# A two-layer hybrid decoder trunk on one core: the first weight unit split in halves by VectorE, and the last rows' order

## What is computed

```python
def rms_norm(x, g):
    y = x * rsqrt(mean(x * x, axis=-1, keepdims=True) + 1e-6)
    return y * g

for l in range(2):
    h = h + token_mixer(rms_norm(h, ln1_g[l]), w_in[l], ...)   # z = u @ w_in: 12 small units, then 16 of gates
    h = h + hier_moe(rms_norm(h, ln2_g[l]), ...)               # top-1 group, top-2 of 32 experts
return rms_norm(h, final_g)
```

## Time and profile before

| | |
|---|---|
| median of 3 runs | 1491.13 us (1489.23 to 1492.70) |
| the profiled execution | 1488.76 us |
| its span, first to last instruction | 1487.0 us |
| TensorE busy | 1401.3 us, 94% of the span |
| VectorE, ScalarE, GpSimd busy | 432.0, 474.9, 493.5 us |
| moved from and to memory | 232 GB/s over the span |
| chain that ended last | TensorE 77%, DMA 17%, VectorE 2%, ScalarE 1%, GpSimd 1% |

### The profile page before, as it was taken

One profiled execution on the slowest core, in us unless ns is written; L12 is line 12 of the kernel. 1 busy time (PEld: TensorE's weight loads), 2 busy tenths in 40 slices (PEclk: granted clock), 3 DMA queues, 4 the chain that ended last, 5 costly groups with the idle time before them and its releaser, 6 DMA issues.

```text
span 1487.0 us, 19004 instructions
## 1 busy us (share of the span) xinstructions
PE 1401.3 (94%) x7518; PEld 979.8 (66%) x7518; DVE 432.0 (29%) x1042; ACT 474.9 (32%) x818; POOL 493.5 (33%) x241
## 2 busy tenths in 40 slices
PE   5999999999999898988899999999999999988986
PEld 5888877788888633333388888777888875333333
DVE  3232544411122311111233335443112142121114
ACT  4522466632331111111244325666223311111112
POOL 3634433456660111111154342335566401111101
PEclk9999999999999799999999999999999998999999
DMA  6522222224375899999963223222243669999996
GB/s 239 197 86 70 87 71 72 71 72 162 106 258 206 334 409 420 419 420 416 389 233 109 78 64 101 77 72 71 71 163 129 238 237 410 415 421 419 420 414 260
DMA packets 128978, 331.22 MB, mean 223 GB/s; under 512 B 16469, under 2 KB 90245, under 8 KB 105336
## 3 DMA queue, kind: packets, MB, share of 16 engines
q1 hardware_dynamic: 120248, 314.28, 55.8%
q0 software_dynamic: 8640, 15.69, 2.8%
HBM read 312.16 MB, written 33.55 MB: 232 GB/s over the span
## 4 chain that ended last, share of the span: by engine, by line
PE 77%; DMA 17%; DVE 2%; ACT 1%; SPq 1%; issue 1%; POOL 1%; POOLq 0%; DVEq 0%; ACTq 0%
PE ps L556 18%; PE ps L557 17%; PE ps L558 17%; PE ps L939 13%; DMA w<-in_w 12%; DMA yb<-y_dram 2%; PE ps L753 2%; DMA x_dram<-hs 1%; PE ps L733 1%; PE ps L741 1%; PE ps L931 1%; DMA xg<-x_dram,toks 1%; PE ps L689 1%; SPq L455 1%; PE ps L850 1%
## 5 line engine op out<-in xcount | busy, mean ns | idle before, releaser
L556 PE MATMUL ps<-uH,ringH 128*128 128x512 f32 x720 | 282.0, 392 | 0.0
L557 PE MATMUL ps<-uL,ringH 128*128 128x512 f32 x720 | 280.5, 390 | 0.0
L558 PE MATMUL ps<-uH,ringL 128*128 128x512 f32 x720 | 280.3, 389 | 0.0
L939 PE MATMUL ps<-w,xT 128*64 128x512 f32 x1024 | 228.0, 597 | 16.0 <-DMA w<-in_w 13.5
L939 PEld LDWEIGHTS ps<-w,xT 128*64 128x64 f32 x1024 | 77.7, 138 | 161.4 <-issue 152.0
L1349 POOL TENSOR_TENSOR ringL<-raw,ringH 128x2048 fp32r<-128x2048 f32 (+1 forms) x31 | 137.9, 4458 | 82.9 <-ACT ringH L1079 82.9
L939 PE MATMUL ps<-w,hT 128*64 128x512 f32 x512 | 127.0, 642 | 31.3 <-DMA w<-in_w 19.5
L556 PEld LDWEIGHTS ps<-uH,ringH 128*128 128x128 f32 x720 | 135.2, 188 | 28.9 <-issue 0.7
L558 PEld LDWEIGHTS ps<-uH,ringL 128*128 128x128 f32 x720 | 135.2, 188 | 28.5
L557 PEld LDWEIGHTS ps<-uL,ringH 128*128 128x128 f32 x720 | 135.3, 188 | 27.6
L1395 POOL TENSOR_TENSOR ringL<-raw,ringH 128x2048 fp32r<-128x2048 f32 x32 | 146.9, 4592 | 5.4 <-ACT ringH L1220 5.4
(11 more groups left out here) (260 smaller groups left out, 2074.0 us busy)
## 6 DMA issues: line engine op xcount, KB each, us to landing
w<-in_w SPq DMA_DIRECT2D x176, 1024.0 KB, 17.9
raw<-in_w_in SPq DMA_DIRECT2D x54, 1024.0 KB, 5.2
w<-in_w SPq DMA_DIRECT2D x32, 512.0 KB, 17.9
braw<-in_w_branch SPq DMA_DIRECT2D x32, 256.0 KB, 4.4
raw<-in_w_out SPq DMA_DIRECT2D x8, 1024.0 KB, 5.2
yb<-y_dram SPq DMA_DIRECT2D x8, 1024.0 KB, 16.0
h_dram<-hs SPq DMA_DIRECT2D x2, 2048.0 KB, 11.3
y_dram<-attT SPq DMA_DIRECT2D x8, 512.0 KB, 8.5
```

The source lines that it names most:

```text
L556: mm(o, h, rh, start=first, stop=False)
L557: mm(o, h, rl_, start=False, stop=False)
L558: return mm(o, l, rh, start=False, stop=last)
L939: ins = mm(o[r], lhs[:, r], rhs[x], start=first, stop=last, skip_group_check=True)
```

## The change

Front: SyncE loads `g1` ahead of weight unit 0. TensorE issues six identity products (`keep_warm(6, 5)`) once `cst` is there, transposes tile 0, issues five more, and starts tile 0's product; the transposes of tiles 1, 2, 3 move to the middle (k = 4) of the products of tiles 0, 1, 2. For unit 0, TensorE waits for the first half of the low part before the product and for the second half only at k = 4. ScalarE makes the high part of unit 0 in two halves of 1024 columns, with `norm_h(0)` and squares 1 between them, and `split_h(2)` comes ahead of `norm_h(3)`. VectorE makes the low part of unit 0 in two halves (`unit_low_half`), GpSimd no longer does. End: the mean of tile 0 is made ahead of tile 1's additions, tile 3's scaling and store are cut in two halves of 512 columns, and TensorE issues four products of banks 2 and 3 ahead of bank 1's wait. Layer 1's front is unchanged.

```diff
--- before.py
+++ after.py
@@ -268,7 +268,7 @@
     bank_filled = signal("bank_filled", NH + 40)
     NB0, NB1 = (NH + 1) // 2, NH // 2
     bank_freed = [signal("bank_freed0", NB0 + 20), signal("bank_freed1", NB1 + 20)]
-    front_high = signal("front_high", 1); front_low = signal("front_low", 1)
+    front_high = signal("front_high", 1, 1); front_low = signal("front_low", 1, 1)
     side_turned = signal("side_turned", 2); side_copied = signal("side_copied", 2)
     lowrank_ready = signal("lowrank_ready", 1)
     decay_arg = signal("decay_arg", 1)
@@ -359,8 +359,8 @@
     def _(sp):
         sp.dma_start(hs[:, 0, :], a["x"][0, 0:P, :]).then_inc(x_in[0].h, 16)
         sp.dma_start(cst[:], a["c_small"]).then_inc(cst_in.h, 16)
+        sp.dma_start(g1[:], a["ln1_g"][0:1, :].partition_broadcast(P)).then_inc(g1_in.h, 16)
         sp.dma_start(raw[:, 0, :].rearrange("p (k n) -> p k n", k=KD), w_in_cols(0, COL["gv"], 256)).then_inc(w_in_slot[0].h, 16)
-        sp.dma_start(g1[:], a["ln1_g"][0:1, :].partition_broadcast(P)).then_inc(g1_in.h, 16)
         for t in range(1, NT):
             sp.dma_start(hs[:, t, :], a["x"][0, t * P:(t + 1) * P, :]).then_inc(x_in[t].h, 16)
 
@@ -542,8 +542,13 @@
         hold(sp, h_out.h, 16 * L)
         for t in range(NT):
             hold(sp, rows_normed.h, rows_normed.at(L, t + 1))
-            sp.dma_start(out[0, t * P:(t + 1) * P, :], ut[:, t, :]).then_inc(s_out.h, 16)
-        hold(sp, s_out.h, 16 * NT)
+            if t < NT - 1:
+                sp.dma_start(out[0, t * P:(t + 1) * P, :], ut[:, t, :]).then_inc(s_out.h, 16)
+        for c in range(2):
+            cc = slice(c * 512, (c + 1) * 512)
+            hold(sp, rows_normed.h, rows_normed.at(L, NT + c))
+            sp.dma_start(out[0, (NT - 1) * P:S, cc], ut[:, NT - 1, cc]).then_inc(s_out.h, 16)
+        hold(sp, s_out.h, 16 * (NT + 1))
 
 
 
@@ -567,7 +572,13 @@
             pe.wait_ge(y_back[t].h, y_back[t].at(lay, 16))
             mm(bank(SUM_BANKS[x]), ident, yb[t][:, 1, cc], start=False, stop=True, skip_group_check=True).then_inc(sum_filled.h, 1)
 
+        def keep_warm(n, b):
+
+            for _ in range(n):
+                mm(bank(b, 256), ident, cst[:, 0:256], start=True, stop=True)
+
         pe.wait_ge(cst_in.h, 16)
+        keep_warm(6, 5)
         for lay in range(L):
 
             def norm_transposes(n, dst_free):
@@ -584,7 +595,7 @@
 
             norm_transposes(0, rows_low)
             if lay == 0:
-                norm_transposes(1, rows_low)
+                keep_warm(5, 5)
             else:
                 token_rows(5, 0, True, False)
                 token_rows(5, 1, False, False)
@@ -592,12 +603,11 @@
                 other_rows(lay - 1, 5)
 
             def second_tile():
-                if lay:
-                    norm_transposes(1, rows_low)
-                    for x in (6, 7):
-                        token_rows(x, 0, True, False)
-                        token_rows(x, 1, False, False)
-                        other_rows(lay - 1, x)
+                norm_transposes(1, rows_low)
+                for x in (6, 7):
+                    token_rows(x, 0, True, False)
+                    token_rows(x, 1, False, False)
+                    other_rows(lay - 1, x)
                 norm_transposes(2, rows_low)
 
             def half(q):
@@ -606,8 +616,9 @@
                 n = UNITS[u][1]
                 wH = ringH[:, s, 0:KD * n].rearrange("p (k n) -> p k n", k=KD)
                 wL = ringL[:, s, 0:KD * n].rearrange("p (k n) -> p k n", k=KD)
-                pe.wait_ge(unit_low.h, unit_low.at(lay, u + 1))
-                if u == 0 and lay:
+                if u or lay:
+                    pe.wait_ge(unit_low.h, unit_low.at(lay, u + 1))
+                if u == 0:
                     pe.wait_ge(front_low.h, front_low.at(lay - 1, 1))
                 if q >= 2:
                     pe.wait_ge(bank_freed[b].h, bank_freed[b].at(lay, q // 2))
@@ -618,14 +629,16 @@
                 else:
                     for i in range(2):
                         if q < 2:
-                            if q == 0 and i == 1:
+                            if q == 0 and i == 1 and lay:
                                 second_tile()
-                            if q == 1 and i == 0 and lay == 0:
-                                norm_transposes(3, rows_low)
                             hold(pe, rows_low.h, rows_low.at(lay, 2 * q + i + 1))
                         for k in range(KD):
                             if q == 1 and i == 0 and k == 4 and lay:
                                 norm_transposes(3, rows_low)
+                            if q < 2 and 2 * q + i < 3 and k == 4 and lay == 0:
+                                norm_transposes(2 * q + i + 1, rows_low)
+                                if q == i == 0:
+                                    pe.wait_ge(unit_low.h, unit_low.at(0, 1))
                             last = mm3(ps[:, b * 512 + i * n:b * 512 + (i + 1) * n], uH[:, k, tmc(2 * off + i)],
                                        uL[:, k, tmc(2 * off + i)], wH[:, k, :], wL[:, k, :], k == 0, k == KD - 1)
                 last.then_inc(bank_filled.h, 1)
@@ -914,15 +927,10 @@
             def list_weights(rhs):
                 return list_product(lambda x: rhs[:, x].rearrange("p a e -> p (a e)"), 384, 2 * NP)
 
-            def keep_warm(n):
-
-                for _ in range(n):
-                    mm(bank(A[0], 256), ident, cst[:, 0:256], start=True, stop=True)
-
-            keep_warm(2)
+            keep_warm(2, A[0])
             pe.wait_ge(list_weights_ready.h, list_weights_ready.at(lay, 1))
             list_weights(w_rhs).then_inc(list_weights_filled.h, 1)
-            keep_warm(6)
+            keep_warm(6, A[0])
 
 
             def transpose_rows(src):
@@ -977,8 +985,11 @@
                 hold(pe, tokens_ready.h, tokens_ready.at(lay, 2))
                 for x in range(2 * NT if lay + 1 == L else 5):
                     if x < 2:
+                        if x and lay + 1 == L:
+                            token_rows(2, 0, True, False)
+                            token_rows(3, 0, True, False)
                         hold(pe, last_low.h, last_low.at(lay, x + 2))
-                    else:
+                    elif lay + 1 < L or x > 3:
                         token_rows(x, 0, True, False)
                     if lay + 1 == L and x < 4:
                         token_rows(x, 1, False, True).then_inc(sum_filled.h, 1)
@@ -1101,11 +1112,13 @@
 
             row_squares(0)
             if lay == 0:
+                act.wait_ge(w_in_slot[0].h, w_in_slot[0].at(0, 16))
+                fn(ringH[:, 0, 0:1024], raw[:, 0, 0:1024], ACT.Copy).then_inc(front_high.h, 1)
+                norm_h(0)
                 row_squares(1)
-                split_h(0)
+                fn(ringH[:, 0, 1024:2048], raw[:, 0, 1024:2048], ACT.Copy).then_inc(unit_high.h, 1)
                 row_squares(2)
                 row_squares(3)
-                norm_h(0)
                 norm_h(1)
             else:
                 norm_h(0)
@@ -1119,6 +1132,7 @@
             split_h(1)
             if lay == 0:
                 norm_h(2)
+                split_h(2)
                 norm_h(3)
 
             def k2_rows(br):
@@ -1158,7 +1172,7 @@
 
             for q in range(NH):
                 kind, u, off, name = HALVES[q]
-                if q == 0 or HALVES[q - 1][1] != u:
+                if (q == 0 and lay) or (q and HALVES[q - 1][1] != u):
                     split_h(u + 2)
                 if name == "ga":
                     act.wait_ge(s_cst.h, 16 * N_CST)
@@ -1354,8 +1368,6 @@
 
             for t in range(NT):
                 norm_scale(t)
-                if lay == 0 and t == 1:
-                    split_l(0)
             split_l(1)
             if lay == 0:
                 hold(pool, s_cst.h, 16 * N_CST)
@@ -1491,10 +1503,27 @@
             v.tensor_tensor(uL[:, :, tmc(t)], ps[:, b * 512:b * 512 + 1024].rearrange("p (k n) -> p k n", k=KD),
                             uH[:, :, tmc(t)].bitcast(f32), ALU.subtract).then_inc(rows_low.h, 1)
 
+        def unit_low_half(c):
+
+            cc = slice(c * 1024, (c + 1) * 1024)
+            if c == 0:
+                dve.wait_ge(front_high.h, front_high.at(-1, 1))
+            else:
+                dve.wait_ge(unit_high.h, unit_high.at(0, 1))
+            v.tensor_tensor(ringL[:, 0, cc], raw[:, 0, cc], ringH[:, 0, cc].bitcast(f32), ALU.subtract).then_inc((front_low, unit_low)[c].h, 1)
+
         mean_square(0, 0)
         first_rows(0, 0)
+        unit_low_half(0)
+        norm_low(0, 0)
         mean_square(0, 1)
         first_rows(0, 1)
+        mean_square(0, 2)
+        unit_low_half(1)
+        first_rows(0, 2)
+        norm_low(0, 1)
+        mean_square(0, 3)
+        first_rows(0, 3)
 
         for lay in range(L):
             links = [0]
@@ -1507,12 +1536,6 @@
 
 
             if lay == 0:
-                norm_low(0, 0)
-                mean_square(0, 2)
```

(13 more changed lines are left out.)

## The result

The changed kernel took 1495.76 us, the median of 11 runs (1492.76 to 1498.80), beside 1490.40 us for the kernel before in 11 runs (1488.26 to 1494.33): a ratio of 1.0036, 95% interval 1.0026 to 1.0046. It is **5.4 us slower**, where 2.9 us faster was forecast; the range ended at 1490.4. The profiled execution took 1494.09 us with a span of 1492.3, against 1488.76 and 1487.0.

A forecast was written before the change was run, and what follows sets the result against it. TensorE, busy without a gap from 36 to 311 us, was taken as the bound, its beginning held by scaled rows and weights. Front 2.1 plus end 0.75 made 2.9 us: 1488.2 against the 1491.13 median, range 1486.2 to 1490.4.

The forecast's parts named there:

- The extra cold identity products: Front: TensorE's identity products ahead of tile 0's product, claimed to cost nothing if they end before 14.8 us.
- they are worth nothing: End: TensorE's four reordered products fill a wait of their own; the banks are full before VectorE asks, so no gain.
- rival 5: Front: TensorE, with waits between tiles, stays at the low clock until tile 3; +6.9 - 0.75, 1497.3 us; chance 0.04.
- Front, 2.1 us: Kernel start: product begins at 14.8 instead of 20.3 us, waits between tiles eat the rest; -2.1 us (-1.6 to -2.6).
- rival 1: Front: GpSimd's factor 2 delays VectorE's second low half by 0.55 us; gain 2.35, 1488.8 us; chance 0.12.
- Rival 3: Front: scaling 3 avoids GpSimd's collision at 1.28 us, tile 2 starts 0.65 earlier; gain 3.55, 1487.6 us; chance 0.10.
- Rival 4: Front: weights or unit 2 land late, each 1 us costing 1 us; at 1.5, 1489.7 us; chance 0.08.
- should arrive at 311 us unchanged: From 36 to 311 us TensorE is busy without a gap, so an earlier beginning should carry through whole.
- End, 0.75 us: Last rows: earlier mean plus halved last scaling and store, -0.75 us together (-0.15 to -0.8).
- The order: End: tile 0's mean ahead of tile 1's additions starts scaling 0 0.2 us earlier, kept to the end.
- The halved store: End: half of the 2.6 us landing is transfer, so halving saves up to 0.65; 0.6 taken, bounds 0 and 0.65.
- rival 2: Front: transposes don't raise the clock, so the product starts 1.9 us late; gain 1.9, 1489.3 us; chance 0.16.

The follow-up runs named there:

- experiment 3: The kernel before with only the front's edits, identity products included, the end as before: 1494.53 us, ratio 1.0024.
- experiment 2: The kernel before with only the edits of the last rows (mean's order, four early products, halved scaling and store), TensorE's code unmoved: 1490.63 us, ratio 0.9998.
- experiment 6: The changed kernel with 64 satisfied waits in layer 0 where TensorE waits for weights, later code moved 106 in all: 1489.87 us, ratio 0.9984.
- experiment 12: The changed kernel with 32 satisfied waits in layer 0 where TensorE waits for weights, later code moved 74 in all: 1493.97 us, ratio 1.0008.
- experiment 7: The changed kernel with six wider identity products instead of eleven, so later code moves by 23 instructions: 1496.32 us, ratio 1.0034.
- experiment 8: Experiment 6 with GpSimd's low half of unit 1 in layer 0 held back until VectorE has scaled tile 3: 1491.77 us, ratio 0.9998.

## Why the prediction was wrong

**The step that failed** is two sentences: "The extra cold identity products cost nothing as long as they end before 14.8", and of the tail, "they are worth nothing". Each was weighed by TensorE's time where the products stand. Neither sum asks what else their instructions change. The first set moves TensorE's code by 43 instructions and brings a jump of about 4 us instead of 0.4 at each of two places, 2.0 us lost in layer 0 and 0.9 in layer 1 (experiment 3; 2.4 in layer 0 of the changed kernel). The second costs nothing in experiment 2, where they fill a wait of 0.76 us for `yL`, and about 2 more in layer 1 once TensorE is late and its clock low. None of the five rivals had this; rival 5, the only one on the slow side, had its reason in the front's clock, which was at the upper level.

The sum from the profiles: front -1.2, tail -0.25, jump of layer 0 +2.4, end of layer 1 +2.8 gives +3.8 against a span that is 5.3 longer. Of the other 1.5, 1.1 lie at the identity products ahead of the experts, which run at the lower level (5.47 us instead of 4.10); that was seen, not tried, and the rest was not traced.

**Front, 2.1 us.** Right in mechanism, and some 0.6 too high: 1.17 in the two profiles compared, 1.5 between the averages. From ScalarE's first instruction on unit 0 to the second bank's copy it is 23.28 us in four profiles, those of the changed kernel and of experiments 3, 6 and 12 (11.84 to 35.12, 11.09 to 34.37, 10.70 to 33.98, 11.71 to 34.99). The forecast has 22.8 (11.2 to the bank's end at 33.8, and 0.2 for the copy); 0.44 of the 0.5 more is VectorE's wait for the factor, which takes 1.36 us instead of 0.55 beside the low half, rival 1's effect. The weights' landing, taken as 11.2, was between 10.6 and 11.8: that is the spread of 0.6 up and down, from 1.2 to 2.3 us of gain, against the one profile of the kernel before, in the profiles with identity products. Rival 3 was mispriced: with the collision missed 0.34 comes back, not 0.65, since `norm_low(2)` then waits for TensorE's transposes. Rival 4's cause (weights late) was in the profiled run with 0.6 of its 1.5 us. The prediction also says that whatever the front gains "should arrive at 311 us unchanged". In the changed kernel it did (1.17 to 498 us); in the profiles of experiments 3, 6 and 7 it did not, about 3 us were lost at 147 to 157 us (last section).

**End, 0.75 us.** 0.25 in its place. The order gave 0.25 as forecast (0.2). The halved store, put at 0.6 by half of a landing of 2.6 us, gave nothing; the low bound of 0 was right. No row showed that half of the landing is transfer. The landing did get 0.5 us shorter with half of the bytes (2.1 us); the later issue and the longer way from landing to end took it back.

**The whole, without the moved code**, is what experiment 6 measures: 0.9984 (0.9972 to 0.9996), 2.4 us by the ratio (0.6 to 4.2; 1.7 by the medians), beside the 2.9 forecast. It is the only kernel that shows a gain: experiment 8, with its code in the same place, has 0.9998 (0.9986 to 1.0010), and in the profile of experiment 6 the front's 2.3 us are gone by 157 us. So a net gain of the change is likely small and not shown beyond doubt; what is shown is that without the stops the change is not slower. The result was wrong by 8 us. The range, built from the bounds of named steps, had no place for a cost that belongs to none. (Added up again, the bounds give 1487.7 to 1489.4 us, not 1487.5 to 1489.3, and rival 2's gain of 1.9 gives 1489.2; neither matters here.) A chance of 0.04 for slower was far too small for a change that puts some forty instructions ahead of 15,000.

## What to carry to other kernels

Count the instructions that a change adds or takes away on each engine, and look for the jumps behind them: a change can pay for itself where it stands and lose more at a jump 700 us later. The sign is an "issue" wait right behind a jump that the kernel before does not have; the proof is the kernel before with satisfied waits in place of the change, put where the engine waits anyway. Try a few shifts before a change is given up: here 0, 9 and 106 did not delay the next squares, and 23 to 74 delayed them by 2.0 to 5.7 us in layer 0 and by 0 to 2.8 in layer 1.

## What the hardware showed besides

- The jump over the empty loop costs 0.4 us with its target's block there and 3 to 5.9 us without; 0 to 4.6 us of that are seen as idle TensorE.
- A wait on a semaphore that has long been reached costs TensorE about 0.16 us (64 of them 10.2 us in experiment 6; each also raised a semaphore).
- Behind a stretch of 2.4 us of idle the granted clock read 0.50, the level of 1.2 GHz, and each product of 512 columns took 0.43 us instead of 0.23 (layer 1 of the changed kernel). In experiments 3, 6 and 7 it also reads 0.51 to 0.53 from 147 to 153.8 us, where TensorE was busy without a gap; the row of experiment 6, with 32 matmuls where the kernel before has 61:

```profile
147.00:153.80 6.80, 6.80 (x32) 5.95 (x32) 1.85 (x5) 3.34 (x5) 1.49 (x1) 0.52 0.15 52
```

  It takes back about 3 us, all of the front's gain, in those runs (ScalarE's offset goes from -2.3 at 36 us to +0.8 at 157 in experiment 6), and is in neither the profile of before nor that of the changed kernel. It goes with an early front: the clock reads 0.51 to 0.53 where the second bank's copy stood at 33.98 to 34.37 us, 0.75 in experiment 8 (34.29), and 1.00 in the changed kernel (35.12) and experiment 12 (34.99). Its cause stays open.
- GpSimd's 128x1 factor takes 1.36 us instead of 0.55 beside a VectorE subtraction with two operands in SBUF, and VectorE's scaling 3.40 instead of 1.28 beside GpSimd's subtraction.
